# Forgetting attention with one whole-row minimum a row, masks of whole rows made by GpSimd, 512-wide scalings and another split of the copies

## The chip, the cores and the metric

The kernel runs on one core of one Trainium2 chip. The metric is the device time of one execution in microseconds. The kernel before took 2978.84 us (median of three runs, 2965.72 to 2980.3). The profile comes from one further look at one execution, whose first and last instruction are 2974.8 us apart.

## The reference, cut to what matters

The model is a decoder trunk of two layers on 1024 tokens: an RWKV-7 layer, then a layer with forgetting attention, both with memory attention, an output projection and a SwiGLU network. The change touches the forgetting attention of the second layer alone. It has 12 heads of 64 and is swept in blocks of 128 queries:

```python
for blk in range(t // BLOCK_Q):
    q0 = blk * BLOCK_Q
    q1 = q0 + BLOCK_Q
    s = jnp.einsum('bqhd,bkhd->bhqk', q[:, q0:q1], k[:, :q1]).astype(jnp.float32) * ATTN_SCALE
    s = s + c_h[:, :, q0:q1, None] - c_h[:, :, None, :q1]
    causal = jnp.arange(q1)[None, :] <= (q0 + jnp.arange(BLOCK_Q))[:, None]
    s = jnp.where(causal, s, NEG_INF)
    p = jax.nn.softmax(s, axis=-1).astype(v.dtype)
    outs.append(jnp.einsum('bhqk,bkhd->bqhd', p, v[:, :q1]))
```

The result is then multiplied by a gate. A block t sees 128 (t + 1) keys, and only its last 128 keys need the causal mask.

## The kernel before, in words

The program is a chain of phases, each with its own semaphores and all engines' parts written out in order. The forgetting attention is the phase `phase_fox`. The 12 heads are handled as 6 pairs, and each pair as 8 units (one query block of both heads) in the order t = 7, 3, 6, 2, 5, 1, 4, 0, so that wide blocks (t of 4 and more) and narrow ones take turns. There are 48 units; n counts them, h is the head in the pair (0 or 1).

The loops run over rounds i. TensorE (PE) in round i: `scores(i)` (L2431) writes the scores of both heads into PSUM banks 0 to 3; `turn(i-1, 0)` transposes the probabilities of head 0 of the unit before into banks 4 and 5 (L2455 and L2459 for a wide unit, L2467 for a narrow one); `values(i-2)` (L2445) multiplies transposed probabilities and values into bank 6; `turn(i-1, 1)` follows. After every fourth unit `spread_shares` (L2473) broadcasts the softmax's eight reciprocal sums into bank 7 with 8 small matmuls.

`scores(i)` waits for `lowest`, that is until VectorE (DVE) has read both rows of unit i-1 out of PSUM; there is one set of score banks. DVE adds scores and decay, writes the sum into `prob` and takes the row's minimum in one instruction with an accumulator (the signs are turned round, so the minimum serves as the softmax's maximum). It needs two such instructions a row: L2544 over the keys ahead of the last block, against `decay`, and L2547 over the last 128 keys, against `decay_masked`, started from the minimum of the first. `decay` is a loaded 128 x 1024 tile a head in one of two buffers. A link, a semaphore between the two, makes the second wait for the first. ScalarE (ACT) then takes the exponential of the row (L2514), with the sum in `total`.

The transposed probabilities are copied from PSUM into `prob_t` by two engines: of a wide unit DVE copies tiles 0 to 3 (bank 4, L2556) and ACT the rest (bank 5, L2499); of a narrow unit DVE copies head 0 (L2559) and ACT head 1 (L2502). After every fourth unit DVE takes the reciprocal of `total` (L2563, at the end of the round after), multiplies the spread shares with the gates (L2528, at the head of the next round, four pieces of 128) and, at that round's end, multiplies bank 6 with this scale into `x_res` (L2570, four pieces of 128).

GpSimd (POOL) has one job: 16 masks of 128 x 128 a pair (L2415), made at once for the pair, in two buffers by pair. SyncE loads the next pair's operands two pairs ahead of their last use.

Of the kernel before, what the change touches and what calls it, by code (L numbers as in the profile page):

```python
# [20 lines left out]
ALU = mybir.AluOpType  # L21
# [5 lines left out]
P = 128  # L27
# [79 lines left out]
class Program:  # L107
# [2246 lines left out]
    def phase_fox(self):  # L2354
        nc, ps = self.nc, self.ps
        with ExitStack() as ctx:
# [4 lines left out]
            v = [x.rearrange("p (a c) -> p a c", a=TT) for x in v]  # L2361
            decay_masked = sb("decay_masked", [P, 2, 2, T])
# [4 lines left out]
            qk_in, rest_in, masked, mem_in = sg("qk_in"), sg("rest_in"), sg("masked"), sg("mem_in")  # L2367
            scored, lowest, exped = sg("scored"), sg("lowest"), sg("exped")
# [10 lines left out]
            turns = lambda n: sum(2 if wide(m) else 1 for m in range(n))  # L2379

# [24 lines left out]
            @block.gpsimd  # L2405
            def _(pool):
                future = self.const("future")
                for p in range(PAIRS):
                    rest_wait(pool, p)
                    if p >= 2:  # L2410
                        pool.wait_ge(lowest, 2 * TT * (p - 1))
                    for _, t in units[TT * p:TT * (p + 1)]:
                        at = slice(t * P, (t + 1) * P)
                        for h in range(2):
                            nc.gpsimd.tensor_tensor(decay_masked[:, p % 2, h, at], decay[p % 2][:, h, at], future, ALU.add).then_inc(masked, 1)  # L2415

            @block.tensor
            def _(pe):
                mmul = nc.tensor.matmul

                def scores(n):
                    p, t = units[n]
                    b = p % 2
                    if n % TT == 0:
                        pe.wait_ge(qk_in if p else self.fox_first, 32 * max(p, 1))
                    nk = (t + 1) * P
                    pe.wait_ge(lowest, 2 * n)
                    for c in range(0, nk, HALF):
                        w = min(HALF, nk - c)
                        for h in range(2):  # L2430
                            mm = mmul(ps[:, 2 * h + c // HALF, 0:w], q[b][hs[h], t * P:(t + 1) * P], k[b][hs[h], c:c + w], start=True, stop=True)  # L2431
                    mm.then_inc(scored, 1)

                def values(n):
                    p, t = units[n]
                    b = p % 2
                    if n % TT == 0:
                        rest_wait(pe, p)
                    pe.wait_ge(copied_d, turns(n + 1))
                    pe.wait_ge(copied_a, turns(n + 1))  # L2440
                    if n % 4 == 0:
                        pe.wait_ge(stored, n // 4)
                    for j in range(t + 1):
                        for h in range(2):
                            mm = mmul(ps[hs[h], 6, n % 4 * P:(n % 4 + 1) * P], v[b][:, j, hs[h]], prob_t[:, n % 2, h, j, :], start=(j == 0), stop=(j == t))  # L2445
                    if n % 4 == 3:
                        mm.then_inc(summed, 1)

                def turn(n, h):
                    p, t = units[n]  # L2450
                    pe.wait_ge(exped, 2 * n + h + 1)
                    if wide(n):
                        pe.wait_ge(copied_d, turns(n) + h)
                        for j in range(4):
# [3 lines left out]
                        for j in range(4, t + 1):  # L2458
                            mm = nc.tensor.transpose(ps[:, 5, (j - 4) * P:(j - 3) * P], prob[:, n % 2, h, j * P:(j + 1) * P], self.const("ident"))  # L2459
# [17 lines left out]
                for i in range(N + 2):  # L2477
# [4 lines left out]
                    if i >= 2:  # L2482
                        values(i - 2)
                    if 1 <= i <= N:
                        turn(i - 1, 1)
                        if i % 4 == 0:
                            spread_shares(i // 4 - 1)

            @block.scalar
            def _(act):  # L2490
                flat = lambda x: x.rearrange("p a c -> p (a c)")

                def turned_copy(n, h):
# [3 lines left out]
                    if wide(n):  # L2497
                        act.wait_ge(turned_a, turns(n) + h + 1)
                        nc.scalar.activation(flat(prob_t[:, n % 2, h, 4:t + 1, :]), ps[:, 5, 0:(t - 3) * P], ACT.Copy).then_inc(copied_a, 1)  # L2499
# [4 lines left out]
                for i in range(N + 1):  # L2504
                    for h in range(2):
                        if i >= 1:
                            turned_copy(i - 1, h)
                        if i < N:
                            n, nk = i, (units[i][1] + 1) * P
                            act.wait_ge(lowest, 2 * n + h + 1)  # L2510
                            if n >= 8 and n % 4 == 0 and h == 0:
                                act.wait_ge(shared, n // 4 - 1)
                            u = 2 * (n % 4) + h
# [4 lines left out]
            def _(dve):  # L2518
                link = self.linker(dve, self.vector_link)
                flat = lambda x: x.rearrange("p a c -> p (a c)")  # L2520
                for i in range(N + 3):
                    n = i - 2
                    if 0 <= n < N and n % 4 == 3:
                        p, t = units[n]
                        dve.wait_ge(spread, n // 4 + 1)

                        for m in range(4):
                            last = nc.vector.tensor_tensor(scale[:, n // 4 % 2, m * P:(m + 1) * P], ps[:, 7, m * P:(m + 1) * P],  # L2528
                                                           gate[p % 2][:, units[n - 3 + m][1] * P:(units[n - 3 + m][1] + 1) * P], ALU.mult)
                        last.then_inc(scaled, 1)  # L2530
                    n = i
                    if n < N:
                        p, t = units[n]
                        nk = (t + 1) * P
                        dve.wait_ge(masked, 2 * (n + 1))
                        dve.wait_ge(scored, n + 1)
                        if n >= 2:
                            dve.wait_ge(turned_d, turns(n - 1))
                            dve.wait_ge(turned_a, turns(n - 1))
                    for h in range(2):  # L2540
                        if n < N:
                            s = self.bank2(h)
                            if t:
                                link(nc.vector.tensor_tensor_reduce(  # L2544
                                    out=prob[:, n % 2, h, 0:nk - P], in0=s[:, 0:nk - P], in1=decay[p % 2][:, h, 0:nk - P], scale=1.0, scalar=3e38,
                                    op0=ALU.add, op1=ALU.min, accum_out=least[:, n % 2, h, 0:1]))
                            nc.vector.tensor_tensor_reduce(  # L2547
                                out=prob[:, n % 2, h, nk - P:nk], in0=s[:, nk - P:nk], in1=decay_masked[:, p % 2, h, nk - P:nk], scale=1.0,
                                scalar=least[:, n % 2, h, 0:1] if t else 3e38, op0=ALU.add, op1=ALU.min,
                                accum_out=least[:, n % 2, h, 1:2]).then_inc(lowest, 1)  # L2550
                        m = n - 1
                        if 0 <= m < N:
                            tm = units[m][1]
                            if wide(m):
                                dve.wait_ge(turned_d, turns(m) + h + 1)
                                nc.vector.tensor_copy(flat(prob_t[:, m % 2, h, 0:4, :]), ps[:, 4, :]).then_inc(copied_d, 1)  # L2556
                            elif h == 0:
                                dve.wait_ge(turned_d, turns(m) + 1)
                                nc.vector.tensor_copy(flat(prob_t[:, m % 2, h, 0:tm + 1, :]), ps[:, 4, 0:(tm + 1) * P]).then_inc(copied_d, 1)  # L2559
                    n = i - 1  # L2560
                    if 0 <= n < N and n % 4 == 3:
                        dve.wait_ge(exped, 2 * n + 2)
                        nc.vector.reciprocal(share[:, n // 4 % 2, :], total[:, n // 4 % 2, :]).then_inc(shared, 1)  # L2563
                    n = i - 2
                    if 0 <= n < N and n % 4 == 3:
                        p, t = units[n]
                        dve.wait_ge(summed, n // 4 + 1)
                        dve.wait_ge(scaled, n // 4 + 1)
                        for m in range(4):
                            last = nc.vector.tensor_tensor(self.X[:, p, units[n - 3 + m][1] * P:(units[n - 3 + m][1] + 1) * P], ps[:, 6, m * P:(m + 1) * P],  # L2570
                                                           scale[:, n // 4 % 2, m * P:(m + 1) * P], ALU.mult)
                        last.then_inc(stored, 1)
# [887 lines left out]
```

## Time and profile before

| What | Value |
|---|---|
| Device time, median of 3 runs | 2978.84 us (2965.72 to 2980.3) |
| The profiled execution, first to last instruction | 2974.8 us |
| Difference of the two, taken as what lies around the span | 4.0 us |
| Busy over the span: PE, DVE, ACT, POOL | 2791.2, 1870.3, 1201.8, 1305.4 us |
| The attention phase, first score to last store | 1948.29 to 2164.82 us |
| In it: PE, DVE, ACT, POOL busy | 191.25, 150.16, 108.26, 39.91 us |

The profiled execution's own device time is not listed apart from its span. The phase is 7% of the span. In the rows, "x4" behind a group is a count of instructions, and what stands in brackets is how long the engine was idle before the group and what it waited for. A matmul's end is modelled, so consecutive matmuls overlap a little in the rows. "CUSTOM_DVE_ANT_0" is the instruction with the minimum; the accumulator's read of 84 ns starts before its end.

### The profile page before, as it was taken

Reading aid. Unit: us, or ns where it says so; the run is one execution under the profiler, and the core shown is the slowest. Engines: PE = TensorE matmul, PEld = TensorE weight load, DVE = VectorE, ACT = ScalarE, POOL = GpSimd, SP = SyncE. Lnnn points to the kernel's source line nnn. Section 1 sums busy time; section 2 is a strip of 40 time slices with the busy share of each in tenths; the row PEclk is TensorE's granted clock in tenths of the full one; section 3 lists DMA queues with packets and bytes.
Section 4 is the critical chain, followed back from the end, with each engine's and each line's share of the span. In section 5 each row is a group of like instructions: output and inputs, shape, how many; then the busy total and the mean of one; then the engine's idle time right before and its main releaser. Section 6 shows DMA issues by size and latency. Waiting matters only on the chain. (4 is left out here: it accounts for less than half of the span.)

```text
span 2974.8 us, 56716 instructions
## 1 busy us (share of the span) xinstructions
PE 2791.2 (94%) x23069; PEld 2243.1 (75%) x23069; DVE 1870.3 (63%) x2527; ACT 1201.8 (40%) x2178; POOL 1305.4 (44%) x1112
## 2 busy tenths in 40 slices
PE   7999989999799999998999999988889999999998
PEld 5888777777667788887887777756667788887787
DVE  6333566666443756556986788867752865556895
ACT  3111343333233433334444766545542433334442
POOL 6344234444232545456554454422112555556653
PEclk9999899999799999999999999999999999999999
DMA  5333100010031233336543232342122233335651
GB/s 199 107 100 105 59 25 24 25 46 4 24 127 65 78 128 113 114 114 205 161 123 93 57 100 89 109 164 86 65 78 86 77 119 106 110 114 174 191 142 68
DMA packets 290602, 295.37 MB, mean 99 GB/s; under 512 B 11623, under 2 KB 223709, under 8 KB 289193
## 3 DMA queue, kind: packets, MB, share of 16 engines
q1 hardware_dynamic: 288440, 286.89, 30.6%
q10 hardware_dynamic: 1424, 4.83, 0.4%
q8 instruction: 185, 3.03, 0.4%
q14 instruction: 73, 0.59, 0.1%
q0 software_dynamic: 480, 0.03, 0.0%
HBM read 200.30 MB, written 88.65 MB: 97 GB/s over the span
## 5 line engine op out<-in xcount | busy, mean ns | idle before, releaser
L312 POOL TENSOR_TENSOR w_lo_b<-w_raw_b,w_hi_b 128x512 fp32r<-128x512 f32 (+3 forms) x540 | 748.0, 1388 | 672.8 <-ACT w_hi_b L346 669.5
L396 PE MATMUL ps<-b_hi,w_hi_b 128*128 128x512 f32 x1540 | 610.4, 396 | 9.2 <-issue 9.2
L396 PE MATMUL ps<-b_lo,w_hi_b 128*128 128x512 f32 x1540 | 602.7, 391 | 0.0
L396 PE MATMUL ps<-b_hi,w_lo_b 128*128 128x512 f32 x1540 | 602.3, 391 | 0.0
L346 ACT ACTIVATE w_hi_b<-w_raw_b 128x512 fp32r<-128x512 f32 (+3 forms) x498 | 295.2, 596 | 454.9 <-PE ps L3370 198.1
L396 PEld LDWEIGHTS ps<-b_hi,w_hi_b 128*128 128x128 f32 x1540 | 291.4, 189 | 74.7 <-issue 14.2
L396 PEld LDWEIGHTS ps<-b_lo,w_hi_b 128*128 128x128 f32 x1540 | 291.4, 189 | 63.9 <-issue 3.9
L396 PEld LDWEIGHTS ps<-b_hi,w_lo_b 128*128 128x128 f32 x1540 | 291.1, 189 | 61.1
L3370 PE MATMUL ps<-b_hi,w_hi_b 128*128 128x512 f32 x616 | 245.9, 399 | 24.3 <-DVE x_res L3187 23.8
L3370 PE MATMUL ps<-b_lo,w_hi_b 128*128 128x512 f32 x616 | 242.6, 394 | 0.0
L3370 PE MATMUL ps<-b_hi,w_lo_b 128*128 128x512 f32 x616 | 242.5, 394 | 0.0
L2079 POOL TENSOR_TENSOR join<-lab,consts_sb 128x256 f32<-128x256 f32 x120 | 100.7, 841 | 275.5 <-DVE lab L2239 149.1
L2974 ACT ACTIVATE x_res<-ps 128x512 f32<-128x512 f32 (+1 forms) x172 | 103.7, 603 | 199.6 <-PE ps L396 199.6
L3187 DVE TENSOR_TENSOR x_res<-x_res,ps 128x512 f32<-128x512 f32 x196 | 133.2, 681 | 59.5 <-PE ps L3370 57.7
L312 POOL TENSOR_TENSOR w_lo_b<-w_sum_b,w_hi_b 128x512 fp32r<-128x512 f32 (+3 forms) x83 | 111.2, 1339 | 134.4 <-ACT w_hi_b L346 134.2
L3370 PEld LDWEIGHTS ps<-b_hi,w_hi_b 128*128 128x128 f32 x616 | 117.3, 190 | 60.2 <-DVE x_res L3187 36.7
L3226 DVE TENSOR_TENSOR x_res<-x_res,ps 128x512 f32<-128x512 f32 x42 | 28.9, 688 | 199.2 <-PE ps L396 199.2
L3370 PEld LDWEIGHTS ps<-b_hi,w_lo_b 128*128 128x128 f32 x616 | 117.3, 190 | 25.0
L3370 PEld LDWEIGHTS ps<-b_lo,w_hi_b 128*128 128x128 f32 x616 | 117.4, 191 | 23.6
L368 PE MATMUL ps<-h_hi_a,w_hi_a 128*128 128x512 f32 x368 | 119.5, 406 | 10.5 <-DVE h_lo_a L623 10.5
L308 POOL CAST w_hi_b<-w_raw_b 128x512 fp32r<-128x512 f32 x42 | 27.5, 655 | 226.2 <-POOLq L2578 118.0
L325 DVE TENSOR_TENSOR w_sum_b<-w_raw_b 128x512 f32<-128x512 f32 (+3 forms) x83 | 113.1, 1362 | 6.7 <-DVE w_raw_b L321 0.5
(429 smaller groups left out, 5786.6 us busy)
## 6 DMA issues: line engine op xcount, KB each, us to landing
w_raw_b<-in_w_gate_up SPq DMA_DIRECT2D x88, 512.0 KB, 4.3
act_dram<-x_res SPq DMA_DIRECT2D x44, 512.0 KB, 6.1
sum_dram<-x_res SPq DMA_DIRECT2D x40, 512.0 KB, 2.9
w_raw_b<-in_w_down SPq DMA_DIRECT2D x28, 512.0 KB, 5.8
stage<-sum_dram SPq DMA_DIRECT2D x54, 256.0 KB, 3.8
stage<-act_dram SPq DMA_DIRECT2D x50, 256.0 KB, 4.2
w_raw_a<-in_a_w_in SPq DMA_DIRECT2D x23, 512.0 KB, 4.7
u_dram<-evac_a SPq DMA_DIRECT2D x16, 512.0 KB, 3.0
```

The costliest lines, as they stand in the source:

```text
L308: nc.gpsimd.tensor_copy(self.whi[:, r, 0:n, :], source).then_inc(self.w_hi, 1)
L312: nc.gpsimd.tensor_tensor(self.wlo[:, r, 0:n, :], source, self.whi[:, r, 0:n, :].bitcast(F32), ALU.subtract).then_inc(self.w_lo, 1)
L325: self.nc.vector.tensor_tensor(s2, s1, a11, ALU.subtract).then_inc(self.w_sum, 1)
L346: self.nc.scalar.activation(self.whi[:, j % RING, 0:unit.sizes[b], :], self.block_source(j), ACT.Copy).then_inc(self.w_cast, 1)
L368: mm = nc.tensor.matmul(bank[:, banks + part, 0:n], w[:, j % RING, i, :], operand(lo, k, part), start=(k == 0 and a == 0 and lo == 0), sto ...
L396: mm = self.nc.tensor.matmul(self.ps[:, bank, :], w[:, r, k, :], h[:, block, k, :], start=(start and k == 0 and a == 0 and h is self.bh), ...
L2079: nc.gpsimd.tensor_tensor(join[:, l - 1], lab[:, n % 2], mask(f"join{l}", 4), ALU.mult).then_inc(join_done, 1)
L2974: copy = lambda out, x: nc.scalar.activation(out, x, ACT.Copy)
L3187: tt(x, x, ps[:, base(FT + 1 + v) + bank, :], ALU.add).then_inc(self.psum_free, 1)
L3226: tt(up(f)[:, 1, :], up(f)[:, 1, :], ps[:, b, :], ALU.add).then_inc(summed, 1)
L3370: mm = mmul(ps[:, bank, :], w[:, j % RING, i, :], h[:, b, slot(c), :], start=(start and i == 0 and a == 0 and h is bh), stop=(stop and i = ...
```

## The change

Five edits, all in `phase_fox`.

1. One minimum a row: DVE takes the whole row of 128 (t + 1) keys in one instruction (L2542 of the new code), against a whole masked row. The link is gone. The wait for the mask is now one a head.
2. Whole masked rows: POOL fills `future` once (896 columns of zero and the causal block, L2418 and L2419), and then adds decay and the right end of `future` over the whole row, 16 instructions a pair of 128 to 1024 columns (L2426). Its buffers change with the unit, so that a row of unit n waits for the minimum of unit n-2.
3. The scaling by shares and gates and the scaling into `x_res` are one 512-wide instruction each for four units, in place of four of 128. The four results stand in bank 6 and 7 in descending places so that this can be written.
4. The reciprocal goes to right behind the first row's minimum of the round, and `spread_shares` a round later, between `values` and `turn(i-1, 1)`. DVE's scaling stands behind the second minimum of that round.
5. Of the transposed tiles of a wide unit DVE copies 4, 3, 2, 2 for t = 7, 6, 5, 4 (before: 4 each), and ACT the rest (4, 4, 4, 3; before 4, 3, 2, 1).

```diff
-            future = self.const("future")
-            for p in range(PAIRS):
...
-                    if p >= 2:
-                        pool.wait_ge(lowest, 2 * TT * (p - 1))
...
+                nc.gpsimd.memset(future[:, 0:T - P], 0.0)
+                link(nc.gpsimd.tensor_copy(future[:, T - P:T], self.const("future")))
+                for n, (p, t) in enumerate(units):
+                    if n % TT == 0:
+                        rest_wait(pool, p)
+                    for h in range(2):
+                        if n >= 2:
+                            pool.wait_ge(reduced, reductions(n - 2, h))
+                        nc.gpsimd.tensor_tensor(decay_masked[:, n % 2, h, 0:keys(n)], decay[p % 2][:, h, 0:keys(n)],
+                                                future[:, T - keys(n):T], ALU.add).then_inc(masked, 1)
...
+            by_dve = lambda n: {7: 4, 6: 3, 5: 2, 4: 2}[units[n][1]]
...
+                        if i % 4 == 1:
+                            spread_shares(i // 4 - 1)
                     if 1 <= i <= N:
                         turn(i - 1, 1)
-                        if i % 4 == 0:
-                            spread_shares(i // 4 - 1)
...
+                    dve.wait_ge(masked, 2 * n + h + 1)
+                    nc.vector.tensor_tensor_reduce(
+                        out=prob[:, n % 2, h, 0:keys(n)], in0=row(n, h), in1=decay_masked[:, n % 2, h, 0:keys(n)], scale=1.0,
+                        scalar=3e38, op0=ALU.add, op1=ALU.min, accum_out=least[:, n % 2, h, 1:2]).then_inc(reduced, 1)
...
+                for i in range(N + 2):
+                    if i < N:
+                        reduce(i, 0)
+                    if ends_four(i - 1):
...
+                        nc.vector.reciprocal(share[:, n // 4 % 2, :], total[:, n // 4 % 2, :]).then_inc(shared, 1)
+                    if 1 <= i <= N:
+                        turned_copy(i - 1, 0)
+                    if i < N:
+                        reduce(i, 1)
+                    if ends_four(i - 2):
...
+                        nc.vector.tensor_tensor(as_tiles(scale[:, n // 4 % 2, :]), as_tiles(ps[:, 7, :]), four_tiles(gate[p % 2], n), ALU.mult).then_inc(scaled, 1)
+                    if 1 <= i <= N:
+                        turned_copy(i - 1, 1)
...
+                        nc.vector.tensor_tensor(four_tiles(self.X[:, p, :], n), as_tiles(ps[:, 6, :]), as_tiles(scale[:, n // 4 % 2, :]), ALU.mult).then_inc(stored, 1)
```

PE, from the second turn of t = 2 to the scores of t = 4, before:

```order
7372 L2467 MATMUL ps<-consts_sb,fox_prob 128x128 x3
7373 L2473 MATMUL ps<-consts_sb,fox_share 64x128 x8
7374 L2431 MATMUL ps<-b_hi 128x256 x2
7375 L2455 MATMUL ps<-consts_sb,fox_prob 128x128 x4
7376 L2459 MATMUL ps<-consts_sb,fox_prob 128x128 x2
7377 L2445 MATMUL ps<-fox_prob_t,b_hi 64x128 x6
7378 L2455 MATMUL ps<-consts_sb,fox_prob 128x128 x4
7379 L2459 MATMUL ps<-consts_sb,fox_prob 128x128 x2
7380 L2431 MATMUL ps<-b_hi 128x512 x2
```

The same stretch now:

```order
7372 L2480 MATMUL ps<-consts_sb,fox_prob 128x128 x3
7373 L2443 MATMUL ps<-b_hi 128x256 x2
7374 L2468 MATMUL ps<-consts_sb,fox_prob 128x128 x2
7375 L2472 MATMUL ps<-consts_sb,fox_prob 128x128 x4
7376 L2457 MATMUL ps<-fox_prob_t,b_hi 64x128 x6
7377 L2486 MATMUL ps<-consts_sb,fox_share 64x128 x8
7378 L2468 MATMUL ps<-consts_sb,fox_prob 128x128 x2
7379 L2472 MATMUL ps<-consts_sb,fox_prob 128x128 x4
7380 L2443 MATMUL ps<-b_hi 128x512 x2
```

The eight spread matmuls have moved from ahead of the next unit's scores to behind `values` of that round, and the turned tiles of t = 5 are split 2 and 4 where they were 4 and 2.

DVE, the round of t = 5 and the one after up to its first minimum, before ("ISA" is the minimum, or with 128x1 the read of its accumulator):

```order
1368 L2544 ISA fox_prob,fox_least<-ps,b_hi 128x640
1369 L2544 ISA fox_least 128x1
1370 L2547 ISA fox_prob,fox_least<-ps,fox_decay_masked,fox_least 128x128
1371 L2547 ISA fox_least 128x1
1372 L2559 COPY fox_prob_t<-ps 128x384
1373 L2544 ISA fox_prob,fox_least<-ps,b_hi 128x640
1374 L2544 ISA fox_least 128x1
1375 L2547 ISA fox_prob,fox_least<-ps,fox_decay_masked,fox_least 128x128
1376 L2547 ISA fox_least 128x1
1377 L2563 RECIPROCAL fox_share<-fox_total 128x8
1378 L2528 TENSOR_TENSOR fox_scale<-ps,b_hi 128x128 x4
1379 L2544 ISA fox_prob,fox_least<-ps,b_hi 128x128
```

The same now, up to the scaling:

```order
1352 L2542 ISA fox_prob,fox_least<-ps,fox_decay_masked 128x768
1353 L2542 ISA fox_least 128x1
1354 L2565 RECIPROCAL fox_share<-fox_total 128x8
1355 L2554 COPY fox_prob_t<-ps 128x384
1356 L2542 ISA fox_prob,fox_least<-ps,fox_decay_masked 128x768
1357 L2542 ISA fox_least 128x1
1358 L2542 ISA fox_prob,fox_least<-ps,fox_decay_masked 128x256
1359 L2542 ISA fox_least 128x1
1360 L2551 COPY fox_prob_t<-ps 128x256
1361 L2542 ISA fox_prob,fox_least<-ps,fox_decay_masked 128x256
1362 L2542 ISA fox_least 128x1
1363 L2574 TENSOR_TENSOR fox_scale<-ps,b_hi 128x512
```

A row has one minimum in place of two, the reciprocal stands between the two rows, and the scaling has left the place ahead of the next round's first minimum for the one behind its second.

## Rows read from the trace of the kernel before

**Rows 1.** Busy time by engine: one pair (t = 7 scores to the next), the phase.

```profile
core 0: us, PE busy (x) PEld busy (x) DVE busy (x) ACT busy (x) POOL busy (x), PEclk, DMA share, GB/s
2020.18:2054.94 34.76, 31.12 (x298) 21.02 (x297) 24.98 (x91) 17.84 (x44) 6.66 (x16) 1.00 0.24 92
...
1948.29:2164.82 216.53, 191.25 (x1776) 128.37 (x1776) 150.16 (x540) 108.26 (x265) 39.91 (x96) 0.97 0.26 91
```

**Rows 2.** Timeline of PE in that pair: start, duration, [idle before, releaser].

```profile
2020.18 1.99 PE L2431 MATMUL ps<-b_hi 64*128 64x512 f32 x8
...
2023.60 0.33 PE L2467 MATMUL ps<-consts_sb,fox_prob 128*128 128x128 f32 x1
2025.58 1.09 PE L2473 MATMUL ps<-consts_sb,fox_share 128*64 128x128 f32 x16 [1.65 <-DVE fox_share L2563]
2026.60 1.13 PE L2431 MATMUL ps<-b_hi 64*128 64x512 f32 x4
...
2029.58 0.63 PE L2455 MATMUL ps<-consts_sb,fox_prob 128*128 128x128 f32 x4 [0.46 <-DVE fox_prob_t L2556]
...
2035.78 0.92 PE L2431 MATMUL ps<-b_hi 64*128 64x384 f32 x4 [0.36 <-DVE fox_least L2547]
...
2044.18 1.09 PE L2473 MATMUL ps<-consts_sb,fox_share 128*64 128x128 f32 x16 [0.51 <-DVE fox_share L2563]
...
2052.32 0.49 PE L2431 MATMUL ps<-b_hi 64*128 64x128 f32 x4 [0.43 <-DVE fox_least L2547]
```

**Rows 3.** Timeline of DVE: the same pair, in three of its rounds.

```profile
2022.31 1.09 DVE L2544 CUSTOM_DVE_ANT_0 fox_prob<-ps,b_hi 128x896 f32<-128x896 f32 x1 [1.44 <-PE ps L2431]
...
2023.72 0.28 DVE L2559 COPY fox_prob_t<-ps 128x128 f32<-128x128 f32 x1
...
2025.32 0.20 DVE L2563 RECIPROCAL fox_share<-fox_total 128x8 f32<-128x8 f32 x1
...
2041.18 0.82 DVE L2544 CUSTOM_DVE_ANT_0 fox_prob<-ps,b_hi 128x640 f32<-128x640 f32 x1 [1.23 <-PE ps L2431]
...
2049.83 0.69 DVE L2544 CUSTOM_DVE_ANT_0 fox_prob<-ps,b_hi 128x512 f32<-128x512 f32 x1
```

**Rows 4.** Groups of DVE by shape, 1950 to 2165 us.

```profile
L2556 DVE COPY fox_prob_t<-ps 128x512 f32<-128x512 f32 x48 | 33.1, 690 | 7.9 <-PE ps L2455 7.9
L2547 DVE CUSTOM_DVE_ANT_0 fox_prob<-ps,fox_decay_masked,fox_least 128x128 f32<-128x128 f32 x84 | 29.5, 351 | 3.0
L2544 DVE CUSTOM_DVE_ANT_0 fox_prob<-ps,b_hi 128x896 f32<-128x896 f32 x12 | 13.0, 1087 | 13.6 <-PE ps L2431 7.2 <-POOL fox_decay_masked L2415 6.4
...
L2528 DVE TENSOR_TENSOR fox_scale<-ps,b_hi 128x128 f32<-128x128 f32 x48 | 10.6, 283 | 15.3 <-PE ps L2473 15.3
...
L2544 DVE CUSTOM_DVE_ANT_0 fox_prob<-ps,b_hi 128x128 f32<-128x128 f32 x12 | 3.4, 281 | 0.0
...
L2559 DVE COPY fox_prob_t<-ps 128x384 f32<-128x384 f32 x6 | 3.3, 554 | 0.0
L2559 DVE COPY fox_prob_t<-ps 128x256 f32<-128x256 f32 x6 | 2.5, 421 | 0.0
```

**Rows 5.** Groups of ACT by shape, 1950 to 2165 us.

```profile
L2499 ACT ACTIVATE fox_prob_t<-ps 128x512 f32<-128x512 f32 x12 | 7.2, 597 | 17.0 <-PE ps L2459 17.0
...
L2499 ACT ACTIVATE fox_prob_t<-ps 128x256 f32<-128x256 f32 x12 | 4.6, 385 | 14.8 <-PE ps L2459 14.8
```

**Rows 6.** Groups of POOL by shape, the whole span.

```profile
L312 POOL TENSOR_TENSOR w_lo_b<-w_raw_b,w_hi_b 128x512 fp32r<-128x512 f32 x456 | 668.7, 1468 | 602.8 <-ACT w_hi_b L346 599.5
...
L2415 POOL TENSOR_TENSOR fox_decay_masked<-b_hi,consts_sb 128x128 f32<-128x128 f32 x96 | 39.9, 455 | 134.1 <-DMA b_hi<-u_dram 129.8 <-POOLq L1125 4.3
...
L308 POOL CAST w_hi_b<-w_raw_b 128x512 fp32r<-128x512 f32 x42 | 27.5, 655 | 226.2 <-POOLq L2578 118.0 <-PE ps L368 90.1 <-DMA w_raw_b<-in_w_out 12.8
...
L2099 POOL TENSOR_TENSOR y<-y,bonus 128x1024 f32<-128x1024 f32 x5 | 11.8, 2355 | 0.0
```

**Rows 7.** Timeline of POOL: ahead of the phase, its start, a later pair.

```profile
1939.11 1.29 POOL L312 TENSOR_TENSOR w_lo_b<-w_raw_b,w_hi_b 128x512 fp32r<-128x512 f32 x1
...
1941.75 2.38 POOL L312 TENSOR_TENSOR w_lo_b<-w_raw_b,w_hi_b 128x512 fp32r<-128x512 f32 x1
1948.42 6.63 POOL L2415 TENSOR_TENSOR fox_decay_masked<-b_hi,consts_sb 128x128 f32<-128x128 f32 x16 [4.29 <-POOLq L1125]
...
2042.64 6.66 POOL L2415 TENSOR_TENSOR fox_decay_masked<-b_hi,consts_sb 128x128 f32<-128x128 f32 x16 [27.70 <-DMA b_hi<-u_dram]
```

**Rows 8.** Timeline of DVE: ahead of the phase, and its first rows.

```profile
1941.76 1.23 DVE L1342 TENSOR_TENSOR x_res<-x_res 128x1024 f32<-128x1024 f32 x1
...
1952.23 1.09 DVE L2544 CUSTOM_DVE_ANT_0 fox_prob<-ps,b_hi 128x896 f32<-128x896 f32 x1 [6.41 <-POOL fox_decay_masked L2415]
...
1953.64 1.08 DVE L2544 CUSTOM_DVE_ANT_0 fox_prob<-ps,b_hi 128x896 f32<-128x896 f32 x1
```

More of the change, by code:

```diff
@@ L2361, in phase_fox @@
             v = [x.rearrange("p (a c) -> p a c", a=TT) for x in v]
+            future = sb("future", [P, T])
             decay_masked = sb("decay_masked", [P, 2, 2, T])
@@ L2406, in _ @@
             def _(pool):
-                future = self.const("future")
-                for p in range(PAIRS):
-                    rest_wait(pool, p)
-                    if p >= 2:
-                        pool.wait_ge(lowest, 2 * TT * (p - 1))
[L2412 to L2415, printed above, removed]
+                link = self.linker(pool, future_link)
+                nc.gpsimd.memset(future[:, 0:T - P], 0.0)
[8 more added lines that the diff above has]
+                                                future[:, T - keys(n):T], ALU.add).then_inc(masked, 1)
             @block.tensor
@@ L2425, in scores @@
                         pe.wait_ge(qk_in if p else self.fox_first, 32 * max(p, 1))
[L2426 to L2429, printed above, removed]
+                    if n:
+                        pe.wait_ge(reduced, reductions(n - 1, 1))
+                    for c in range(0, keys(n), HALF):
+                        w = min(HALF, keys(n) - c)
                         for h in range(2):
-                            mm = mmul(ps[:, 2 * h + c // HALF, 0:w], q[b][hs[h], t * P:(t + 1) * P], k[b][hs[h], c:c + w], start=True, stop=True)
+                            mm = mmul(row(n, h)[:, c:c + w], q[b][hs[h], t * P:(t + 1) * P], k[b][hs[h], c:c + w], start=True, stop=True)
                     mm.then_inc(scored, 1)
@@ L2444, in values @@
                         for h in range(2):
-                            mm = mmul(ps[hs[h], 6, n % 4 * P:(n % 4 + 1) * P], v[b][:, j, hs[h]], prob_t[:, n % 2, h, j, :], start=(j == 0), stop=(j == t))
+                            mm = mmul(ps[hs[h], 6, place(n) * P:(place(n) + 1) * P], v[b][:, j, hs[h]], prob_t[:, n % 2, h, j, :], start=(j == 0), stop=(j == t))
                     if n % 4 == 3:
@@ L2452, in turn @@
                     if wide(n):
+                        d = by_dve(n)
                         pe.wait_ge(copied_d, turns(n) + h)
-                        for j in range(4):
+                        for j in range(d):
                             mm = nc.tensor.transpose(ps[:, 4, j * P:(j + 1) * P], prob[:, n % 2, h, j * P:(j + 1) * P], self.const("ident"))
@@ L2518, in _ @@
             def _(dve):
-                link = self.linker(dve, self.vector_link)
                 flat = lambda x: x.rearrange("p a c -> p (a c)")
[L2521 to L2535, printed above, removed]
-                        dve.wait_ge(scored, n + 1)
[L2537 to L2561, printed above, removed]
@@ new lines, in turned_copy @@
+                def turned_copy(m, h):
+                    tm = units[m][1]
+                    if wide(m):
+                        d = by_dve(m)
+                        dve.wait_ge(turned_d, turns(m) + h + 1)
+                        nc.vector.tensor_copy(flat(prob_t[:, m % 2, h, 0:d, :]), ps[:, 4, 0:d * P]).then_inc(copied_d, 1)
+                    elif h == 0:
+                        dve.wait_ge(turned_d, turns(m) + 1)
+                        nc.vector.tensor_copy(flat(prob_t[:, m % 2, h, 0:tm + 1, :]), ps[:, 4, 0:(tm + 1) * P]).then_inc(copied_d, 1)
```

42 lines of the change are left out of this document (28 added, 14 removed).

## The prediction

> **What bounds the kernel now.** I read busy time by stretch first. The attention phase takes 216.53 us [rows 1], 7% of the span, and nothing outside it changes, so the question is what one pair of heads costs: 34.76 us from one t = 7 to the next, six times. In it PE is busy for 31.12 us, DVE for 24.98, ACT for 17.84, POOL for 6.66 [rows 1]. PE is the engine that is nearly full; its work is the same after the change, so 31.12 is the floor of a pair and 34.76 - 31.12 = 3.64 us is all that can be won in one. Then I read PE's timeline of the pair for these 3.64 us, and the reader should see five gaps, every one of which ends on DVE [rows 2]: 1.65 ahead of the spread of shares at t = 7, 0.46 in the round of t = 3 (DVE's copy has not emptied bank 4), 0.36 ahead of the scores of t = 2, 0.51 ahead of the other spread, 0.43 ahead of the scores of t = 0. Together 3.41; the other 0.23 are crumbs. DVE is only 72% busy, but it is the short loop that waits: scores, two minima with a copy between them, next scores. What counts of the change is what it takes out of DVE between a unit's scores and the moment at which its second row has been read.
>
> **The minima.** A pair has 14 rows with two minima. A whole row is one longer instruction: the slope between 128 and 896 columns is (1087 - 281)/768 = 1.05 ns a column [rows 4], so 1024 columns take 1.22 us and 1.26 with the accumulator's read. Before, a row of t = 7 and its link went from 2022.31 to the copy at 2023.72, and two of them with the copy between to 2025.32, where the reciprocal starts [rows 3]. The difference in a row: the second minimum (0.35) and its gap go, 128 columns at 1.05 ns (0.13) come, so 0.22 us less, 0.43 in a round.
>
> **The stalls one by one.** Times are of the pair in rows 2 and 3.
> - t = 7: scores are there at 2022.31 [rows 3]. Two rows of 1.26, a copy of 0.2 and now the reciprocal's 0.2 between them end at 2025.2. PE's own work ends at 2023.60 + 0.33 = 2023.93 [rows 2]; it goes on at 2025.3, a gap of 1.4 in place of 1.65. The reciprocal has moved into the same chain, and this wait was never for the reciprocal alone: next in line there, behind the spread, stood the scores of t = 3, which need the same second row.
> - t = 3: the spread's eight matmuls (1.02 us, from 2025.58 to 2026.60 [rows 2]) now stand where PE waited 0.46 for bank 4. The gap goes to nothing. What they could delay, the second turn and the DVE copy behind the scaling, has a round's slack on DVE: its four-piece scalings shrink too.
> - t = 6: 0.43 less on DVE against a gap of 0.36: about 0.05 is left.
> - t = 5: from 2041.18 [rows 3], two rows of 768 columns (0.95 + 0.04 each), a copy of about 0.5 and the reciprocal's 0.15 end at 2043.8, PE goes on at 2043.9 where it was free at 2043.7: 0.2 in place of 0.51.
> - t = 4: from 2049.83 two rows of 640 (0.82 + 0.04) and a copy of 0.35 end at 2051.9; about 0.1 in place of 0.43.
> - The crumbs stay: 0.2.
> The sum is 1.4 + 0 + 0.05 + 0.2 + 0.1 + 0.2 = 1.95 us of PE idle, against 3.64. That is 1.7 a pair. The freed DVE time elsewhere (below) can only shave the same gaps by a tenth or so: I take 1.8, and 6 x 1.8 = 10.8 us.
>
> **The scalings and the split.** Two 512-wide instructions for eight of 128, twice a pair: four took about 0.88, at 283 ns each [rows 4], overlapping, one takes about what a 512-wide copy from PSUM takes, 0.69. That is 0.19 each, 0.76 a pair of DVE time. The scaling also leaves the place ahead of a unit's first minimum, where PE hides it today. The copies of t = 6, 5, 4 give DVE 2 x (0.14 + 0.27 + 0.27) = 1.35 us back a pair (690 ns to 554 and 421 [rows 4]); ACT takes about 0.11 us a tile (597 - 385 = 212 ns for two [rows 5]), ten tiles a pair, 1.1 us on an engine at 17.84 of 34.76. I cost both at nothing beyond the 0.1 taken above: DVE falls from 24.98 to about 24.98 - 3.0 - 0.76 - 1.35 = 19.9 us a pair, but what lies outside the short loop is idle time already. If ACT's longer copy did delay an exponential, the next `turn` would wait; it has the scores of the next unit (0.5 to 2 us) as cover.
>
> **The masks.** This is the price, and the trace does not show it in place. POOL adds 2 x 36 x 128 = 9216 columns a pair in 16 instructions. By the 128-wide row (455) and the 1024-wide one (2355) [rows 6], an instruction is 0.18 us plus 2.12 ns a column: 22.5 us a pair. By the 1468 ns of 512 columns it is 2.87 ns a column, 26.4 us. Both stay under 33 us a pair. A row's mask may be started two rounds ahead of its use (about 8.5 us), and the two longest neighbours, t = 7 and 3, take 2 x (2.36 + 1.27) = 7.3 us, so I cost it at nothing in the steady part. SyncE's loads are not moved: they wait for `stored`, which comes in the same round. Only the start is bare: from 1948.42 [rows 7] POOL fills `future` (memset of 896 columns: between the 0.1 of nothing and 1.1 us, the 655 ns of the 512-wide cast [rows 6] scaled; I take 0.7), copies 128 columns (0.2), and makes two rows of 2.36. The first is ready at about 1951.8, before the scores (1952.23), the second at 1954.2, where DVE started its second row at 1953.64 [rows 8]. That is 0.6 us lost, between 0 and 2. At the end the spread, now behind the last `values`, is bare: its 1.02 us less the 0.4 for shorter scalings, 0.6. Together 1.2.
>
> **Sum.** 10.8 - 1.2 = 9.6 us less: a span of 2965.2, plus the 4.0 that the median of 2978.84 lies above the profiled span: 2969.2 us, 0.3% faster. No change can be told within about 0.5%, 14.9 us.
>
> **A rule against the change.** The trace shows that a GpSimd instruction can be held up: the 512-wide one that takes 1.29 us took 2.38 at 1941.75 [rows 7], just when DVE ran a 1.23 us square with both inputs in SBUF at 1941.76 [rows 8]. In the attention phase sixteen masks take 6.63 us at the start, where DVE is mostly idle, and 6.66 in a later pair where it is 72% busy [rows 7]: no hold-up. Every large DVE instruction there has an operand in PSUM, and that stays so. The Trainium skill, "SBUF — State Buffer", section "SBUF: two separate sides", says that GpSimd and VectorE share a port pair as an exclusive lock, which a VectorE instruction takes if it has two SBUF inputs or runs in a two-port mode. By that rule nothing is locked here, and the trace agrees in both places; by a plain reading of "they share ports" the second rival would win.
>
> **Rivals.**
> - *All of PE's waits go.* If the chain at t = 7 were shorter than I think, a pair would be 31.12 to 31.9 us: 6 x 3.64 - 1.2 = 20.6 less, 2958 us; from 15 less on it counts as faster. For it: every gap ends on DVE, which loses 5 of 25 us. Against it: two 1024-column rows must follow the scores and PE has 1.75 us of work there. Chance 0.18.
> - *POOL becomes the bound (slower).* If DVE and POOL excluded one another, a pair would take 22.5 + 19.9 = 42.4 us, 7.6 more than now: 6 x 7.6 = 46 slower, 3025 us. It decides from 3.25 ns a column on, where the masks take 33 us a pair. For it: the 2.38 us instruction. Against: the equal 6.63 and 6.66, and PSUM operands. Chance 0.10, from 15 slower on.
> - *The gain is given back inside the phase.* Spread now sits ahead of the second turn, DVE's scaling waits for it and the copy that frees bank 4 stands behind; if each of the 12 spreads cost a 0.8 us delay there, the sum is zero: 2979 us. Against: behind the spread PE still has a turn and the scores of the next wide unit to do before it needs DVE again. Chance 0.12.
>
> **Numbers.** The forecast has 0.60, 2964 to 2975 us. The runs of the kernel before lie 15 us apart, which widens every case. Faster by over 0.5%: 0.18 and a little of the forecast, 0.20. Slower: 0.10. Same: 0.70. The range, 2957 to 2982, takes in the floor and the zero case and leaves out the POOL rival.
>
> **What would show it.** Right: pairs of 32.8 to 33.2 us; PE's one large gap, about 1.4 us, ahead of the scores of t = 3 and ended by the minimum; no wait on the shares; DVE near 20 us a pair; masks of 1024 columns at 2.4 us and DVE not waiting for them after the first unit. Wrong: a DVE wait on masks in every pair, 1024-column masks of over 3.5 us, whole-row minima of more than 1.3 us, or pairs under 32 us.

## The result and the profile after

The changed kernel takes 2958.41 us (median of 12 runs, 2943.41 to 2964.93) against 2974.27 us for the kernel before in its 12 runs (2965.72 to 2984.46). The medians are 15.9 us apart. The ratio is 0.9939, with a 95% interval of 0.9925 to 0.9954: about 18 us, 0.6%, faster. Forecast were 9.6 us, so the gain was 1.7 times the forecast by the medians and 1.9 times by the ratio. The range began at 2957 us, 1.4 us below the measured median. It held the time because it reached down to the rival in which all of PE's waits go, not because the sum was near. The chances were put mainly on "no change that can be told" (0.70); the measured ratio lies on the other side of that bound, though its interval still touches it.

The profile says where it came from. The span fell from 2974.8 to 2956.2 us, by 18.6, and the phase from 216.53 [rows 1] to 198.52, by 18.0. The other 0.6 us lie outside the phase, where no edit was made. Busy time by stretch of the changed kernel, one pair from t = 7 to t = 7 and the phase, answers to rows 1:

```profile
core 0: us, PE busy (x) PEld busy (x) DVE busy (x) ACT busy (x) POOL busy (x), PEclk, DMA share, GB/s
2015.27:2046.76 31.49, 30.50 (x297) 21.08 (x297) 19.59 (x51) 18.77 (x44) 22.07 (x17) 1.00 0.26 101
1948.35:2146.87 198.52, 187.56 (x1776) 128.62 (x1776) 117.99 (x300) 114.04 (x265) 133.41 (x98) 0.97 0.28 99
```

From the second pair on a pair takes 31.49 us in place of 34.76, to within 0.01 us each time. PE's idle time fell from 3.64 to 0.99 us, and, which the prediction had excluded, PE's busy time from 31.12 to 30.50. PE's timeline of that pair has one bracket left (answers to rows 2):

```profile
2018.69 0.33 PE L2480 MATMUL ps<-consts_sb,fox_prob 128*128 128x128 f32 x1
2020.01 1.13 PE L2443 MATMUL ps<-b_hi 64*128 64x512 f32 x4 [0.99 <-DVE fox_least L2542]
...
2022.09 0.44 PE L2457 MATMUL ps<-fox_prob_t,b_hi 128*64 128x128 f32 x4
2022.36 1.04 PE L2486 MATMUL ps<-consts_sb,fox_share 128*64 128x128 f32 x16
2023.33 0.66 PE L2468 MATMUL ps<-consts_sb,fox_prob 128*128 128x128 f32 x4
```

And DVE's timeline of the t = 7 round (answers to rows 3):

```profile
2017.31 1.23 DVE L2542 CUSTOM_DVE_ANT_0 fox_prob<-ps,fox_decay_masked 128x1024 f32<-128x1024 f32 x1 [1.83 <-PE ps L2443]
...
2018.46 0.20 DVE L2565 RECIPROCAL fox_share<-fox_total 128x8 f32<-128x8 f32 x1
2018.57 0.24 DVE L2554 COPY fox_prob_t<-ps 128x128 f32<-128x128 f32 x1
2018.73 1.22 DVE L2542 CUSTOM_DVE_ANT_0 fox_prob<-ps,fox_decay_masked 128x1024 f32<-128x1024 f32 x1
```

The reader should look at the starts. A row of 1024 columns lasts 1.23 us, but the reciprocal starts 1.15 after it, the copy 0.11 after that, the next row 0.16 later. From the first row's start to the end of the second it is 2.64 us.

The masks cost what the prediction said. Groups of POOL by shape, 1940 to 2160 us (answers to rows 6):

```profile
L2426 POOL TENSOR_TENSOR fox_decay_masked<-b_hi,fox_future 128x1024 f32<-128x1024 f32 x12 | 28.0, 2360 | 19.5 <-DVE fox_least L2542 19.4
L2426 POOL TENSOR_TENSOR fox_decay_masked<-b_hi,fox_future 128x896 f32<-128x896 f32 x12 | 24.9, 2094 | 0.0
...
L2426 POOL TENSOR_TENSOR fox_decay_masked<-b_hi,fox_future 128x128 f32<-128x128 f32 x12 | 5.2, 461 | 0.0
```

POOL's timeline at the phase's start (answers to rows 7):

```profile
1948.61 0.84 POOL L2418 MEMSET fox_future<- 128x896 f32 x1 [4.27 <-POOLq L1125]
1949.40 0.29 POOL L2419 COPY fox_future<-consts_sb 128x128 f32<-128x128 f32 x1
```

DVE's timeline there, the second row of the first unit (answers to rows 8):

```profile
1954.45 1.22 DVE L2542 CUSTOM_DVE_ANT_0 fox_prob<-ps,fox_decay_masked 128x1024 f32<-128x1024 f32 x1 [0.95 <-POOL fox_decay_masked L2426]
```

From the first mask on it is POOL that waits for DVE; this row is the only one in the phase for which DVE waits for POOL.

### The profile page after: what moved, and what is told of

It is laid out like the page before. It is cut to its first block and busy times, and to the rows that moved or that the text cites. A ratio compares the mean times of both kernels' runs of the same rounds, so it can differ in the third digit from the quotient of the medians.

```text
span 2956.2 us, 56479 instructions
## 1 busy us (share of the span) xinstructions
PE 2783.9 (94%) x23069; PEld 2240.4 (76%) x23069; DVE 1838.7 (62%) x2287; ACT 1207.5 (41%) x2178; POOL 1399.0 (47%) x1114
## 3 DMA queue, kind: packets, MB, share of 16 engines
HBM read 200.30 MB, written 88.65 MB: 98 GB/s over the span
## 5 line engine op out<-in xcount | busy, mean ns | idle before, releaser
L2426 POOL TENSOR_TENSOR fox_decay_masked<-b_hi,fox_future 128x1024 f32<-128x1024 f32 (+7 forms) x96 | 132.3, 1412 | 51.8 <-DVE fox_least L2542 51.5
```

The lines of the kernel that those rows point to most:

```text
L2426: nc.gpsimd.tensor_tensor(decay_masked[:, n % 2, h, 0:keys(n)], decay[p % 2][:, h, 0:keys(n)], future[:, T - keys(n):T], ALU.add).then_inc ...
```

## The experiments

A pair's length, from the scores of one t = 7 to the next, repeats to 0.01 us, while whole executions of one kernel differ by 10 us and more. So do stretches that no edit touches: the phase starts at 1935 us in one kernel and at 1955 in another. Each `b` kernel and a2, a3, a4, c1 and c2 were executed once, so their whole times decide nothing. So the parts are told apart by the pair and the phase. Theory A is the prediction's mechanism, taken at its measured size: PE's idle time is the DVE chain between a unit's scores and its second row, plus waits for bank 4. The rivals are that the moved spread did it, and that DVE's total load binds.

**Parts of the change on the kernel before.** Each `b` kernel is the kernel before with the named edits of the section on the change.

b1_rows, edits 1 and 2 only (a cut: POOL's part is that of the change):

```diff
-                        dve.wait_ge(masked, 2 * (n + 1))
...
+                            dve.wait_ge(masked, 2 * n + h + 1)
+                            nc.vector.tensor_tensor_reduce(
+                                out=prob[:, n % 2, h, 0:nk], in0=s[:, 0:nk], in1=decay_masked[:, n % 2, h, 0:nk], scale=1.0,
+                                scalar=3e38, op0=ALU.add, op1=ALU.min,
```

> The kernel before with one minimum a row and whole masked rows alone; reciprocal, spread, four-piece scalings and the split of the copies as before. Theory A (PE's waits are for the DVE chain between scores and second row, and two minima a row were most of it): the pair goes from 34.76 to about 32.5 us; the gap ahead of the spread at t = 7 from 1.65 to about 1.2, the gaps ahead of the scores of t = 2 and t = 0 to nothing. Rival B (the moved spread and reciprocal bring the gain): over 34 us. Rival C (each edit helps only together with the others): about 34 us, and the parts add up to much less than 3.27.

b2_split, edit 5 only:

```diff
+            by_dve = lambda n: {7: 4, 6: 3, 5: 2, 4: 2}[units[n][1]]
```

> The kernel before with the split of the turned tiles alone (DVE 4, 3, 2, 2). Theory A: the copy stands in the DVE chain of narrow rounds, where PE waits only 0.46 us for bank 4 and 0.36 and 0.43 us behind wide rounds, so little: 34.5 us a pair, DVE 1.3 us less busy. Rival (DVE's total load is what binds): its 1.35 us come back whole, 33.4 us.

b3_order, edit 4 only (a cut: PE's part; DVE's reciprocal and scaling move as in the change):

```diff
                         values(i - 2)
+                        if i % 4 == 1:
+                            spread_shares(i // 4 - 1)
                     if 1 <= i <= N:
                         turn(i - 1, 1)
-                        if i % 4 == 0:
-                            spread_shares(i // 4 - 1)
```

> The kernel before with the order alone: reciprocal behind the first row, spread a round later, scaling behind the second row (still four pieces). Theory A: the gap at t = 7 stays near 1.5 us, since the scores of t = 3 need the same second row, the 0.46 us gap of t = 3 is filled by the spread, the one at t = 5 is 0.4: about 33.9 us a pair. Rival B: both gaps on the shares (1.65 and 0.51) go, about 32.5.

b4_rows_order is b1 and b3 together.

> The kernel before with one minimum a row, whole masked rows and the order, but four-piece scalings and the old split. Theory A: close to the changed kernel, 31.6 to 31.9 us a pair against 31.49; the wide scalings and the split are worth no more than 0.3. Rival (DVE's total load binds): 2.1 us of DVE work more than in the changed kernel, 33.6.

a2_split4 is the changed kernel without edit 5:

```diff
-            by_dve = lambda n: {7: 4, 6: 3, 5: 2, 4: 2}[units[n][1]]
+            by_dve = lambda n: {7: 4, 6: 4, 5: 4, 4: 4}[units[n][1]]
```

> The changed kernel with DVE copying four turned tiles of every wide unit again. Theory A: DVE has slack outside the t = 7 round, so 31.5 to 31.8 us a pair. Rival: 1.35 us more DVE work cost 1.35 us, 32.8.

| Kernel | Edits | Pair, us | PE, DVE busy in it | Phase, us | PE's gaps of over 0.1 us in the pair |
|---|---|---|---|---|---|
| before | none | 34.76 | 31.12, 24.98 | 216.53 | 1.65, 0.46, 0.36, 0.51, 0.43, 0.18 |
| b2_split | 5 | 34.46 | 31.05, 23.61 | 213.80 | 1.65, 0.46, 0.36, 0.51, 0.43 |
| b3_order | 4 | 33.78 | 30.83, 24.67 | 211.23 | 1.60, 0.35, 0.46, 0.35, 0.18 |
| b1_rows | 1, 2 | 32.20 | 30.89, 22.03 | 201.59 | 1.03, 0.18 |
| b4_rows_order | 1, 2, 4 | 31.80 | 30.62, 21.78 | 200.27 | 0.98, 0.18 |
| a2_split4 | 1 to 4 | 31.70 | 30.54, 21.09 | 200.30 | 0.98, 0.18 |
| changed kernel | all | 31.49 | 30.50, 19.59 | 198.52 | 0.99 |

The phases are from one execution each and hold the slow clock of the first pair (it read 0.82 and 0.83 in the changed kernel and before), so they are rougher than the pairs. Read down the last four rows, the whole-row minimum is worth 2.56 of the 3.27 us, the order 0.40 more, the wide scalings 0.10, the split 0.21. These shares depend on the order in which the edits are taken: on the kernel before, the order alone gives 0.98 and the split alone 0.30. Both rivals fall: the order alone is far from all of the gain, and 2.2 us of DVE work a pair (b4 against the changed kernel) are worth 0.31. The expectations by theory A held for the split, the order, b4 and a2; b1_rows came out 0.3 us shorter than expected (32.20 for 32.5), with 1.03 for the gap of 1.2. The order alone behaves as the prediction argued: the gap on the shares goes and the same gap appears on the minimum behind it, PE's timeline of b3_order at t = 7:

```profile
2023.63 1.13 PE L2431 MATMUL ps<-b_hi 64*128 64x512 f32 x4 [1.60 <-DVE fox_least L2539]
```

The split's 0.21 is one gap. In the t = 0 round of a2_split4 PE waits 0.18 us, and its timeline names an exponential of ACT:

```profile
2038.21 0.63 PE L2468 MATMUL ps<-consts_sb,fox_prob 128*128 128x128 f32 x4 [0.18 <-ACT fox_prob L2528]
```

DVE's timeline of the same kernel just ahead of it:

```profile
2037.37 0.69 DVE L2551 COPY fox_prob_t<-ps 128x512 f32<-128x512 f32 x1 [0.28 <-PE ps L2468]
```

That turn also waits for bank 4, which this copy frees at 2038.06, 0.15 us ahead of PE's start. In the kernel before, at t = 3, the distance from the copy's end (2029.44) to PE's start was 0.14. The exponential that the turn needs had ended at 2037.56 in ACT's timeline. With a copy of 256 columns (0.42 us) the gap is gone.

**The t = 7 gap.** a3_recip_late moves the reciprocal behind the second row:

```diff
                         reduce(i, 1)
+                    if ends_four(i - 1):
+                        n = i - 1
+                        dve.wait_ge(exped, 2 * n + 2)
+                        nc.vector.reciprocal(share[:, n // 4 % 2, :], total[:, n // 4 % 2, :]).then_inc(shared, 1)
```

> The changed kernel with the reciprocal behind the second row's minimum. Theory A: everything between the scores of t = 7 and the second row counts one for one; the reciprocal's slot there is 0.11 us, so the gap falls from 0.99 to 0.88 and the pair to 31.38 us. Rival (the gap's end is set by something else, such as the mask of the second row): 31.49 unchanged.

Measured: gap 0.92, pair 31.41, where 0.88 and 31.38 were expected. Without the reciprocal the copy starts 1.15 us behind the first row and the second row 0.20 behind the copy (0.16 with it), so the chain is 2.56 us in place of 2.64. It lost 0.08 us, the gap 0.07 and the pair 0.08: the chain counts one for one.

c1_psum and c2_sbuf add work on DVE between the two rows of t = 6 and t = 4, and differ in its first operand (`ps[:, 7, :]` or the decay tile in SBUF):

```diff
                         reduce(i, 0)
+                    if 6 <= i < N and i % 4 == 2:
+                        nc.vector.tensor_tensor(spare[:, i // 4 % 2, :], ps[:, 7, :], future[:, 0:HALF], ALU.add)
```

> The changed kernel with one more 128x512 addition on DVE in the rounds of t = 6 and t = 4, one operand in PSUM (its result is not used). Control of the next: masks on GpSimd keep their durations (2.36 us for 1024 columns, 1.27 for 512), because no DVE instruction of the phase has both inputs in SBUF. If GpSimd and DVE block each other whatever the operands, the masks that run beside these additions are 0.7 us longer.

> The same addition on DVE in the same rounds, with both inputs in SBUF. If two SBUF inputs are what held a GpSimd instruction up ahead of the phase (2.38 for 1.29 us), masks beside the addition are now up to 0.7 us longer, or the addition waits for the mask and takes up to 3 us, in two rounds a pair; the pair grows by that where it falls into the DVE chain. If the hold-up had another cause, durations as in the control.

Both give pairs of 32.38 us, 0.89 more, with two new gaps of 0.34 and 0.41: the two additions take 0.61 us of DVE's time each, so those rounds had about 0.2 to 0.3 us of slack. Groups of POOL, c1_psum (1937 to 2140 us):

```profile
L2427 POOL TENSOR_TENSOR fox_decay_masked<-b_hi,fox_future 128x1024 f32<-128x1024 f32 x12 | 28.1, 2362 | 19.5 <-DVE fox_least L2543 19.4
...
L2427 POOL TENSOR_TENSOR fox_decay_masked<-b_hi,fox_future 128x768 f32<-128x768 f32 x12 | 21.8, 1824 | 16.4 <-DVE fox_least L2543 16.4
```

and of c2_sbuf (1947 to 2148 us):

```profile
L2427 POOL TENSOR_TENSOR fox_decay_masked<-b_hi,fox_future 128x1024 f32<-128x1024 f32 x12 | 29.6, 2490 | 19.5 <-DVE fox_least L2543 19.4
...
L2427 POOL TENSOR_TENSOR fox_decay_masked<-b_hi,fox_future 128x768 f32<-128x768 f32 x12 | 23.8, 1985 | 14.7 <-DVE fox_least L2543 14.7
```

One addition and the two masks beside it show it directly. In c1_psum the addition starts at 2032.48 in DVE's timeline, and POOL's timeline has:

```profile
2032.71 4.68 POOL L2427 TENSOR_TENSOR fox_decay_masked<-b_hi,fox_future 128x1024 f32<-128x1024 f32 x2 [3.88 <-DVE fox_least L2543]
```

In c2_sbuf the distance is the same, DVE's timeline and then POOL's:

```profile
2042.72 0.69 DVE L2564 TENSOR_TENSOR fox_spare<-b_hi,fox_future 128x512 f32<-128x512 f32 x1
2042.95 5.00 POOL L2427 TENSOR_TENSOR fox_decay_masked<-b_hi,fox_future 128x1024 f32<-128x1024 f32 x2 [3.88 <-DVE fox_least L2543]
```

With a PSUM operand the masks keep their 2360 and 1825 ns; with two SBUF inputs the mask that starts beside the addition is some 0.3 us longer; the means of the two shapes rise by about 0.15 us, so that is about every second mask of them (the longest mask took 2682 ns against 2370 in the control). The addition itself keeps its 0.69 us. Expected were up to 0.7 us; the mask starts 0.23 us behind the addition, so 0.46 us of it were left. In the phase it is thus the operands that decide, and the changed kernel is free of it because every large DVE instruction reads PSUM. This is what the Trainium skill says in "SBUF — State Buffer", section "SBUF: two separate sides": VectorE takes the ports that it shares with GpSimd when it has two SBUF inputs. The hold-up ahead of the phase [rows 7, 8] fits it, but it was larger, 1.09 us beside a 1.23 us instruction, and was not tried itself.

**How much POOL can carry.** a4_pool_256 puts 256 columns more behind each mask:

```diff
                                                 future[:, T - keys(n):T], ALU.add).then_inc(masked, 1)
+                        link(nc.gpsimd.tensor_tensor(spare[:, h, 0:256], decay[p % 2][:, h, 0:256], future[:, 0:256], ALU.add))
```

> The changed kernel with one more 128x256 addition on GpSimd behind each mask (its result is not used), and a semaphore between it and the next. POOL would then have 22.1 + 16 x (0.73 + 0.1) = 35.4 us of work a pair. If masks are hidden only while POOL's work stays below the pair: 35.4 us a pair, POOL without idle time, DVE waiting for masks. If the masks' double buffer is already short of slack at 22 us, more than 36. If the masks are ahead by more than the trace suggests, under 34.

Measured: pairs of 36.29 (the first, with the slow clock; 35.44 in the changed kernel) and 35.00 us, then two of 35.41 in the mean, then 33.26; phase 216.07. DVE's timeline of its third pair has what the changed kernel has not, waits for masks at t = 7:

```profile
2026.50 1.23 DVE L2544 CUSTOM_DVE_ANT_0 fox_prob<-ps,fox_decay_masked 128x1024 f32<-128x1024 f32 x1 [1.97 <-POOL fox_decay_masked L2427]
...
2029.47 1.23 DVE L2544 CUSTOM_DVE_ANT_0 fox_prob<-ps,fox_decay_masked 128x1024 f32<-128x1024 f32 x1 [1.47 <-POOL fox_decay_masked L2427]
```

And POOL never stops. Its timeline has the first mask of the third and of the fourth pair at

```profile
2023.98 2.35 POOL L2427 TENSOR_TENSOR fox_decay_masked<-b_hi,fox_future 128x1024 f32<-128x1024 f32 x1
...
2058.73 2.35 POOL L2427 TENSOR_TENSOR fox_decay_masked<-b_hi,fox_future 128x1024 f32<-128x1024 f32 x1
```

From pair to pair these starts are 34.77, 34.75, 34.75 and 34.81 us apart, and four pairs of PE (1989.32 to 2128.40) take 34.77 in the mean; the single ones only differ in where they fall against POOL. So POOL's bound is real: with 11.7 us of additions more on it (22.07 to 33.75 busy, and about 1 us between instructions) it sets the pair and all of the gain is lost. In pairs 2 to 4 the granted clock also read 0.95, 0.95 and 0.90 where the changed kernel has 1.00. This did not set the pair: POOL's period is the same in pair 5, where the clock read 1.00. The 35.4 us expected were 0.6 too many, since the steps between the instructions cost 1.0 us a pair and not 1.6.

**Filling the last gap.** a1_spread_back puts the spread back where it was; a5_spread_mixed does so only for the four units that end with t = 0:

```diff
-                        if i % 4 == 1:
+                        if i % 8 == 5:
                             spread_shares(i // 4 - 1)
                     if 1 <= i <= N:
                         turn(i - 1, 1)
+                        if i % 8 == 0:
+                            spread_shares(i // 4 - 1)
```

> The changed kernel with the spread of shares back behind the second turn of the round (the reciprocal stays early, the scaling stays a round later). Theory A: PE is free from 2019.02 to 2020.01 at t = 7 and waits for the second row; with the shares ready at 2018.66 the spread's 1.0 us fit into that gap, so the pair falls from 31.49 to about 30.5 us, and the time by 6 us more than the changed kernel's, ratio to before about 0.992. Rival: the spread back in front of the scores delays the scores of t = 3 as it did in the kernel before, and the pair stays at 31.5 or grows to 32.

> The changed kernel itself, beside the others on this chip: 31.49 us a pair, ratio to before 0.994.

> The changed kernel with the spread of the four ending on t = 2... that is, of units 7, 3, 6 and 2, left where the change put it, and the spread of units 5, 1, 4 and 0 back behind the second turn of the next pair's t = 7 round, where PE has its one gap. With both spreads back the pair was 30.90 us; there the spread ahead of the scores of t = 1 cost 0.15 (4.07 us from it to the scores of t = 4, against 3.92 in the changed kernel). Theory A: 30.75 us a pair, ratio to before 0.992. Rival (the two places make no difference beyond t = 7): 30.90.

| Kernel | Pair, us | Phase, us | Ratio to before (95%) |
|---|---|---|---|
| changed kernel, again | 31.48 | 198.60 | 0.9946 (0.9925 to 0.9968) |
| a1_spread_back | 30.90 | 194.33 | 0.9916 (0.9897 to 0.9934) |
| a5_spread_mixed | 30.75 | 193.42 | 0.9923 (0.9897 to 0.995) |

The changed kernel again and a5 came out as expected; a1 was expected at 30.5. With the shares ready early the old place is the better one at t = 7: the spread fills the gap, and the one large bracket is gone. At t = 7 the spread costs nothing there (4.73 us from the scores of t = 7 to those of t = 3, against 4.74). a1 won 0.58 and not 1.0 because the spread also had a use where the change put it. Without it at t = 3, PE waits about 0.1 us for bank 4 again and shows the tail of the matmul before, so that round gives back 0.73 and not 0.97; and the spread ahead of the scores of t = 1 costs 0.15, which a5 saves. Phases say 4 to 5 us less than the changed kernel, 0.14 to 0.17%; the ratios' intervals overlap, so the whole time alone does not show it.

## Why the prediction was wrong

The mechanism, its place and its price on POOL were right; the size was about half. Two steps failed. The floor of a pair took PE's busy time as work that stays, and the chain on DVE was added up from durations that overlap. Point by point, 3.27 us a pair were measured against 1.8:

- *"31.12 is the floor of a pair".* The largest miss, 0.6 us: the busy time fell to 30.50, and a1 and a5 have whole pairs of 30.90 and 30.75. Where PE runs on, a group's last matmul overlaps the next group; where it stops, its tail is alone and counts as busy: the same four `values` matmuls of t = 0 take 0.44 us in the row and the next group starts 0.27 after them in the changed kernel, where before a wait stood behind them. The 0.6 us do not go with the listed gaps alone. The order takes 0.29 of them (before to b3) or 0.27 (b1 to b4), though b4 has as many gaps of over 0.1 us as b1, and a1, with none, reads 30.80. Short hand-overs count too. Counting the 0.6 us as work made both the forecast and the rival "all of PE's waits go" too small.
- *t = 7, "they end at 2025.2 ... a gap of 1.4".* Measured 0.99, 0.4 us less. The step added durations (1.26, 0.2, 0.2) where DVE's instructions overlap: starts are 1.15, 0.11 and 0.16 apart, so the chain is 2.64 us and not 2.9. The prediction had the right rows: 2022.31, 2023.72 and 2025.32 are starts. That is 0.28 of the 0.4. Another 0.09 came from nowhere in the sum: the first row starts 2.04 us behind the start of its scores, before 2.13. b1_rows has 2.03 and b2 and b3 2.13, so it came with edits 1 and 2; which part of them does it was not tried.
- *t = 6, 5 and 4, "0.05 + 0.2 + 0.1".* Measured nothing, by the same two causes in each: 0.35 us.
- *t = 3, the spread fills the 0.46.* The gap went, as forecast, but the spread was not needed for most of it: in b1_rows, with the spread in its old place, PE waits only 0.10 us there (from 2019.98 to 2020.08).
- *"The crumbs stay: 0.2."* They went: 0.18 was the wait for bank 4 behind DVE's 512-wide copy at t = 0, which the split shortens. The split was costed at nothing because DVE had idle time outside the chain; a copy that PE waits for is in a chain too.
- The four misses (0.6, 0.4, 0.35, 0.2) make 1.55 us a pair; with the 1.7 that the sum gave, they are 3.25 of the 3.27 measured.
- *Start and end, 1.2 us.* Six pairs at 3.27 would be 19.6, the phase gave 18.0: 1.6 lost, nearly all of it in the first pair (37.12 to 35.44 us, 1.68 less). From the scores of t = 6 on, that pair gained 1.96 us (24.36 to 22.40), as a steady one does. The rounds of t = 7 and t = 3 took 13.04 us for 12.76, where a steady pair gains 1.31. In them DVE waited 0.95 us for the second mask, so that its second row started 0.81 us later than before (1954.45 for 1953.64; 0.6 were forecast), and the next scores came 7.38 us behind the first against 6.89. There was also less to win: no spread stands there in the first pair, and the granted clock read 0.50 to 0.53 in both kernels, so PE's own work took longer and the 0.46 us gap of t = 3 was not there before either. How much is due to which was not tried. The end cost nearly nothing, where 0.6 were forecast (last pair to last store 37.14 us against 40.35, 3.21 less).
- *"Plus the 4.0".* What lies around the span is 1.8 us (2957.98 us for a span of 2956.2 in the changed kernel); the other 2.2 were the distance of the profiled execution from the median of three. It moved the absolute time, not the gain.
- *The masks at nothing in the steady part.* Right: 22.07 us a pair against 22.5, no wait of DVE after the first unit. The rival on POOL fell; its price is real (a4), but its point of decision, 33 us of masks a pair, belonged to the forecast pair of 33 us, and the measured pair is 31.49.
- *"The gain is given back inside the phase".* It fell: b3 and b4 show the spread's new place gaining.

## What to carry to other kernels

Cost a chain on one engine by the distances between starts in the timeline, not by durations, and do so for every instruction between a wait and its release. Take the busy time of a pipelined engine as work plus a tail for each stop, so the floor lies below it: here 31.12 us of busy time became 30.50 for the same matmuls. When a producer is made early, ask again where its consumer fits best: an independent piece of work belongs into the gap that remains, here the spread behind the second turn of t = 7.

## What the runs showed of the hardware

- DVE starts an instruction before the profile ends the one ahead of it: 1.15 us after the start of a 128x1024 minimum that lasts 1.23, 0.11 after a reciprocal of 0.20, 0.16 after a copy of 0.24.
- A 128x512 DVE addition with both inputs in SBUF lengthened a concurrent GpSimd addition by about 0.3 us; the same with one input in PSUM did not, and DVE's own durations were 687 and 685 ns in the two.
- POOL's adds are linear in the columns: 461 ns for 128, 2094 for 896, 2360 for 1024, with DVE busy for 62% of the pair beside them. A memset of 896 columns took 0.84 us.
- In a4_pool_256 PE's four scores of t = 3, with 512 keys, took 2.08 us behind gaps of 2.69 and 2.70 us and 1.61 behind 2.93. They took 2.08 at the phase's start too, where the granted clock read 0.50, the lower of its two levels; in a4 it read 0.71 from 2029 to 2033 us. They took 1.13 us, at 1.00, the higher level, behind 1.40 in the same kernel's fifth pair and 1.60 in b3_order. No gap between 1.60 and 2.69 us was measured ahead of these scores.
